# First stage of a two-layer diffusion backbone, reordered by K tiles

## The reference

```
sc  = silu(c);  scc = silu(c_ctx)
mod = s @ ada_w[i] + ada_b[i]                 # 6 chunks of 1024: shift, scale, gate, ...
h   = rms_norm(x, norm_mix[i]) * (1 + mod[1]) + mod[0]     # context with scc, latent with sc
proj = h @ w_in                               # 1024 -> 512 (cq) + 256 (ckv) + 32 (kr)
q  = rms_norm(cq, q_norm) @ w_uq
kv = rms_norm(ckv, kv_norm) @ w_ukv           # k_nope and v for 16 heads
kr = rope_2d(kr)                              # on the latent tokens
out = softmax(q k) v @ w_o
```

## Time and profile before

| | |
|---|---|
| median of three timed runs | 1244.3 us (1244.23 to 1246.67) |
| the profiled execution's own time | 1248.4 us |
| its span, first to last instruction | 1246.2 us |
| TensorE busy | 1162.3 us, 93% of the span |
| VectorE busy | 861.5 us, 69% |
| ScalarE busy | 610.2 us, 49% |
| GpSimd busy | 221.4 us, 18% |
| mean granted TensorE clock | 0.976 |

### The profile page before, as it was taken

One profiled execution on the slowest core, in us unless ns is written; L12 is line 12 of the kernel. 1 busy time (PEld: TensorE's weight loads), 2 busy tenths in 40 slices (PEclk: granted clock), 3 DMA queues, 4 the chain that ended last, 5 costly groups with the idle time before them and its releaser, 6 DMA issues.

```text
span 1246.2 us, 19292 instructions
## 1 busy us (share of the span) xinstructions
PE 1162.3 (93%) x6954; PEld 974.1 (78%) x6954; DVE 861.5 (69%) x1255; ACT 610.2 (49%) x1048; POOL 221.4 (18%) x166
## 2 busy tenths in 40 slices
PE   5799999898999999999999799998999897999997
PEld 3577776678988888878888778885777797999996
DVE  0896887975887777774665678885888656555453
ACT  3657887733532223232222555547577445666442
POOL 0201444422100000000111100004975211000010
PEclk9899999999999999999999999999999898999999
DMA  9533222240574555554452142221222243556562
GB/s 380 189 135 118 70 84 86 68 169 1 186 235 172 184 200 200 172 191 144 160 171 68 50 136 68 84 84 47 73 73 72 93 151 115 192 179 190 148 186 72
DMA packets 48175, 168.23 MB, mean 135 GB/s; under 512 B 5232, under 2 KB 6512, under 8 KB 47856
## 3 DMA queue, kind: packets, MB, share of 16 engines
q1 hardware_dynamic: 48112, 167.38, 40.4%
HBM read 166.31 MB, written 1.05 MB: 134 GB/s over the span
## 4 chain that ended last, share of the span: by engine, by line
PE 69%; DVE 16%; ACT 7%; issue 3%; DMA 1%; POOL 1%; SPq 1%; DVEq 0%; ACTq 0%
PE bank L1675 21%; PE bank L1677 20%; PE bank L1676 20%; DVE scratch L1456 5%; DVE w_lo L1087 3%; PE bank L2100 2%; ACT w_hi L607 2%; DMA raw<-in_w_in 1%; ACT scratch L912 1%; PE bank L2133 1%; DVE softmax_max L1258 1%; PE bank L2112 1%; ACT conv_in L909 1%; PE bank L2122 1%; DVE mla_h_lo L1278 1%
## 5 line engine op out<-in xcount | busy, mean ns | idle before, releaser
L1087 DVE TENSOR_TENSOR w_lo<-raw,w_hi 128x1024 fp32r<-128x1024 f32 (+1 forms) x226 | 277.3, 1229 | 159.7 <-ACT w_hi L607 159.5
L607 ACT ACTIVATE w_hi<-raw 128x1024 fp32r<-128x1024 f32 (+1 forms) x226 | 230.8, 1023 | 274.8 <-PE bank L1677 252.8
L1675 PE MATMUL bank<-ffn_h_lo,w_hi 128*128 128x256 f32 (+1 forms) x736 | 246.0, 334 | 9.3 <-DVE ffn_h_lo L1124 5.6
L1676 PE MATMUL bank<-ffn_h_hi,w_hi 128*128 128x256 f32 (+1 forms) x736 | 245.1, 333 | 0.0
L1677 PE MATMUL bank<-ffn_h_hi,w_lo 128*128 128x256 f32 (+1 forms) x736 | 245.0, 333 | 0.0
L1675 PEld LDWEIGHTS bank<-ffn_h_lo,w_hi 128*128 128x128 f32 x736 | 140.2, 191 | 25.2 <-issue 6.0
L1677 PEld LDWEIGHTS bank<-ffn_h_hi,w_lo 128*128 128x128 f32 x736 | 140.3, 191 | 14.5
L1676 PEld LDWEIGHTS bank<-ffn_h_hi,w_hi 128*128 128x128 f32 x736 | 140.3, 191 | 14.5
L462 POOL TENSOR_TENSOR scratch<-scratch 128x512 f32<-128x512 f32 (+1 forms) x24 | 34.6, 1441 | 618.8 <-ACT scratch L616 618.8
L1675 PE MATMUL bank<-ssd_h_lo,w_hi 128*128 128x256 f32 (+2 forms) x360 | 125.6, 349 | 4.5 <-DVE ssd_h_lo L1361 2.3
L1675 PE MATMUL bank<-ffn_hidden_lo,w_hi 128*128 128x256 f32 (+1 forms) x374 | 124.4, 333 | 5.8 <-DVE ffn_hidden_lo L1416 5.8
(11 more groups left out here) (265 smaller groups left out, 2159.2 us busy)
## 6 DMA issues: line engine op xcount, KB each, us to landing
raw<-in_w SPq DMA_DIRECT2D x120, 512.0 KB, 4.3
scratch<-in_vec_w SPq DMA_DIRECT2D x56, 512.0 KB, 3.6
vec_weights<-in_vec_w SPq DMA_DIRECT2D x24, 512.0 KB, 3.6
raw<-in_w_xbc SPq DMA_DIRECT2D x24, 512.0 KB, 3.5
ada_start<-in_ada_w SPq DMA_DIRECT2D x8, 1024.0 KB, 17.2
raw<-in_w_z SPq DMA_DIRECT2D x16, 512.0 KB, 3.5
raw<-in_w_so SPq DMA_DIRECT2D x16, 512.0 KB, 3.5
raw<-in_w SPq DMA_DIRECT2D x16, 384.0 KB, 3.9
```

The source lines that it names most:

```text
L607: A(wh[s % RING][:, 0:c], raw[s % RING][:, 0:c], ACT.Copy).then_inc(w_hi, 1)
L1087: V.tensor_tensor(wl[s % RING][:, 0:c], raw[s % RING][:, 0:c], wh[s % RING][:, 0:c].bitcast(f32), SUB).then_inc(w_lo, 1)
L1675: mm(o, lh, rl, start=first, stop=False)
L1676: mm(o, lh, rh, start=False, stop=False)
```

## The change

The order of the first stage is turned: K tiles outside, output tiles inside.

- adaLN columns are laid out anew: group q holds shift and scale of K tiles 2q and 2q+1. `start_mods(q)` copies the rows, waits for the turn, adds the bias and forms the gain of these two K tiles alone.
- X is loaded first, in two halves; TensorE's sums over X come ahead of all adaLN groups, and VectorE's reciprocal ahead of the first row copy.
- w_in is loaded by K tile: eight blocks of 128x896 in place of seven of 128x1024. All later blocks move by one number in the ring.
- The projection runs K tile by K tile into seven banks (`in_all(k)`, 21 matmuls each), with the adaLN groups and turns between; K tiles 6 and 7 are done last, output tile by output tile.
- In VectorE's list two matvecs stand before the fourth row copy and three behind it. ScalarE's silu of the c rows stands behind H's K tiles 4 and 5. Two weight blocks of the heads are split behind the loop over t.
- astart gets SBUF space of its own beside H, since both are now live together.

```diff
-            ada_start(0)
+            for i in range(2):
+                sp.dma_start(X[:, 4 * i:4 * i + 4, :], a["xT"][:, 4 * i:4 * i + 4, :]).then_inc(x_in[i], 16)
+            ada_start(0)
             sp.dma_start(tab[:, :], a["tab"]).then_inc(inputs_in, 16)
             ada_start(1)
-            sp.dma_start(X[:, :, :], a["xT"]).then_inc(x_in, 16)
             ada_start(2)
             ada_start(3)
+            load(IN, IN, 896, one("w_in", 0))
+            load(IN + 1, IN + 1, 896, one("w_in", 1))
             ada_start(4)
             ada_start(5)
...
+            load(IN + 4, IN + 4, 896, one("w_in", 4))
+            sp.dma_start(crow[:, :, :], a["crow"]).then_inc(crow_in, 16)
+            vec(0, vec_mla[:, 0, :])
+            vec(1, vec_mla[:, 1, :])
+            for t in range(5, 8):
+                load(IN + t, IN + t, 896, one("w_in", t))
```

ScalarE (`start_his(k)` makes the high part of K tile k, as `his_shared` did):

```diff
+            hi(IN, IN)
+            start_his(0)
+            hi(IN + 1, IN + 1)
+            act.wait_ge(in_gain, 1)
+            start_his(1)
+            for q in range(1, 4):
+                act.wait_ge(in_gain, q + 1)
+                start_his(2 * q)
+                start_his(2 * q + 1)
+                if q == 1:
+                    hi(IN + 2, IN + 2)
+                    hi(IN + 3, IN + 3)
+                if q == 2:
+                    hi(IN + 4, IN + 4)
+                    act.wait_ge(crow_in, 16)
+                    A(crow[:, :, :], crow[:, :, :], ACT.Silu).then_inc(crow_silu, 1)
+                    hi(IN + 5, IN + 5)
+                    hi(IN + 6, IN + 6)
+            hi(IN + 7, IN + 7)
+            hi(VB, VB)
+            hi(VB + 1, VB + 1)
...
             for t in range(7):
-                act.wait_ge(w_used, IN + t + 1)
+                if t < 6:
+                    act.wait_ge(in_mm, t + 1)
+                else:
+                    act.wait_ge(w_used, IN + KD)
```

VectorE:

```diff
+            dve.wait_ge(inv, 1)
+            for q in range(4):
+                start_mods(q)
+                start_value(2 * q)
+                if q == 0:
+                    lo(IN, IN)
+                start_low(2 * q)
+                start_low(2 * q + 1)
+                if q == 0:
+                    lo(IN + 1, IN + 1)
+                elif q == 1:
+                    lo(IN + 2, IN + 2)
+                    lo(IN + 3, IN + 3)
+                elif q == 2:
+                    lo(IN + 4, IN + 4)
+                    dve.wait_ge(crow_silu, 1)
+                    matvec_mla(0)
+                    lo(IN + 5, IN + 5)
+                    matvec_mla(1)
+                    lo(IN + 6, IN + 6)
+            matvec_mla(2)
+            lo(IN + 7, IN + 7)
+            matvec_mla(3)
+            lo(VB, VB)
+            matvec_mla(4)
+            lo(VB + 1, VB + 1)
             for t in range(7):
```

TensorE:

```diff
+            def in_all(k):
+
+                pe.wait_ge(w_lo, IN + k + 1)
+                pe.wait_ge(nlo, k + 1)
+                for t in range(7):
+                    if k == 0 and t >= 4:
+                        pe.wait_ge(*((row_cp, t - 3) if t < 6 else (root, 1)))
+                    last = in_part(k, t)
+                last.then_inc(w_used, 1)
+
+            ada_group(0)
+            pe.wait_ge(inputs_in, 16)
+            turn_ready(0)
+            turn()
+            ada_group(1)
+            in_all(0)
+            turn_ready(1)
+            turn()
+            in_all(1)
+            ada_group(2)
+            in_all(2)
+            turn_ready(2)
+            turn()
+            in_all(3)
+            ada_group(3)
+            in_all(4)
+            turn_ready(3)
+            turn()
+            in_all(5)
+            pe.wait_ge(w_lo, IN + KD)
+            for t in range(7):
+                for k in (6, 7):
...
             for g in range(8):
+                if g < 4:
+                    pe.wait_ge(proj_out, g + 3)
+                if 1 <= g < 4:
+                    pe.wait_ge(cq_lo, g)
...
                 if g == 0:
                     b = SQ[2]
+                    pe.wait_ge(cq_lo, KQ)
```

More of the change, by code:

```diff
@@ L93, in block_cols @@
     cols = [1024] * NBLK
+    for n in range(IN, IN + KD):
+        cols[n] = 896
     for n in range(HP, HP + 16):
@@ L734, in _, with start_his @@
-            act.wait_ge(crow_in, 16)
-            A(crow[:, :, :], crow[:, :, :], ACT.Silu).then_inc(crow_silu, 1)
+            def start_his(k):
+                even = k % 2 == 0
+                act.wait_ge(nv, NB[0] + k + 2) if even else act.wait_ge(nx, ODD[0] + k // 2 + 1)
+                for m, c0, c1 in ((1, 0, CTX), (0, CTX, TOK)):
+                    v = T[:, (2 if even else 6) + k // 2 % 2, c0:c1]
+                    if even:
+                        ins = A(Hmh[:, k, c0:c1], v, ACT.Identity, bias=mod[0][:, k, m:m + 1])
+                    else:
+                        ins = A(v, v, ACT.Identity, bias=mod[0][:, k, m:m + 1], scale=gain[0][:, k, m:m + 1])
+                if not even:
+                    ins.then_inc(nodd, 1)
+                    act.wait_ge(nodd, ODD[0] + k // 2 + 1)
+                    ins = A(Hmh[:, k, :], T[:, 6 + k // 2 % 2, :], ACT.Copy)
+                ins.then_inc(nhi, 1)
@@ L748, in _ @@
[L748 removed]
+                    square(2, k, bank[t][:, :])
+                    A(cnh[:, KKV + k, :], bank[t][:, :], ACT.Copy, scale=par[:, PAR["q_norm"] + k:PAR["q_norm"] + k + 1]).then_inc(proj_out, 1)
                 if t == 3:
@@ L1764, in _, with ada_group @@
             pe.wait_ge(silu_c, 1)
-            for g in range(4):
+            pe.wait_ge(ones_set, 3)
+            for k in range(KD):
+                pe.wait_ge(x_sq, k + 1)
+                last = mm(bank[6][:, :], ones[:, :], T[:, k, :], start=k == 0, stop=k == KD - 1)
+            last.then_inc(sum_done, 1)
+            def ada_group(g):
                 if g >= 2:
-                    pe.wait_ge(row_cp, g - 1)
+                    pe.wait_ge(mod_ev, g)
                 for r in range(2):
@@ L1770, in _ @@
                     for q in range(2):
-                        ada(4 * r + 2 * q, astart[:, 4 * g + 2 * r + q, :], bank[4 + g % 2])
-                if g == 0:
-                    pe.wait_ge(inputs_in, 16)
-                    pe.wait_ge(ones_set, 3)
-                if g == 1:
-                    for k in range(KD):
-                        pe.wait_ge(x_sq, k + 1)
-                        last = mm(bank[6][:, :], ones[:, :], T[:, k, :], start=k == 0, stop=k == KD - 1)
-                    last.then_inc(sum_done, 1)
@@ L1799, in _ @@
+            pe.wait_ge(w_lo, IN + KD)
+            for t in range(7):
+                for k in (6, 7):
+                    if t == 0:
+                        pe.wait_ge(nlo, k + 1)
+                    last = in_part(k, t)
+                    if t == 6 and k == 6:
+                        last.then_inc(w_used, 1)
+                last.then_inc(in_mm if t < 6 else w_used, 1)
+                if t in (1, 3):
+                    j = 1 if t == 1 else 2
                     if t == 1:
-                        pe.wait_ge(root, 1)
```

139 lines of the change are left out of this document (64 added, 75 removed).

## The result

The changed kernel takes 1250.5 us (median of 7 runs, 1249.8 to 1255.2); the kernel before took 1244.3 beside it (7 runs, 1242.3 to 1246.7). That is 6.2 us more between the medians. The ratio, which is formed from all runs and not from the two medians, is 1.0062, 95% interval 1.0041 to 1.0083: slower by 0.6%, clear of noise. The forecast was 1251.0. Four of the seven runs of after lie from 1249.8 to 1250.5 and three from 1254.9 to 1255.2. Its profiled execution is one of the long ones: 1255.2 us, with a span of 1253.5. The profiled execution of before, 1248.4 us with a span of 1246.2, is longer than all seven timed runs of before.

The account below looks back on a forecast made before the run. TensorE was taken as the bound from 43.15 us to V's end at 99.71. Terms 32.1 + 12.05 + 15.3 + 8.25 + 10.7 + 23.85, plus clock 4.2, gave 106.4: 6.7 us later, median 1251.0, range 1244 to 1257.

Parts of the forecast that it names:

- my own case: The main forecast, 1251.0 us for the median: chance 0.60, said to span 1247.5 to 1254 alone.
- A: End of K tile 0 in the projection, predicted at 32.1 us.
- B: Third turn, after K tile 1, an adaLN group and K tile 2: A + 12.05 us.
- C: Fourth turn, B + 15.3 us: TensorE stands still 3.3 us, the row copy being queued behind two matvecs.
- F: Start of the last two K tiles, C + 8.25 us, after TensorE stands still another 3.05 us for weights 7.
- The opening: Loads to first projection matmul: sums over X end at 16.0 us, matmul at 25.65, 17.5 us earlier than before.
- The clock: Half-clock stretches of 3.4 us behind idles, costing 1.7 us each: 1.7 charged at F, 2.5 at V.
- One to one behind V: Behind V only buffer numbers are edited, so V's 6.7 us delay carries unchanged into the total.
- Rival 1: Clock holds and sums run at full speed: V ends at 100.9, 1.2 us later, 1245.5; chance 0.12.
- Rival 3: Longer half stretches, sums at half speed throughout or two at F: 10 to 12 us later, 1255; chance 0.13.
- Rival 2: TensorE stays the bound, vector chain much shorter: V ends at 85.3, 1230, case put at 1238; chance 0.10.
- Rival 4: Clock falls at every K tile: four stretches of 1.7 us more, 6.8 on top, 1258; chance 0.05.

Follow-up runs that it names:

- experiment 8: Changed kernel with 12 unused matmuls of ones on ones ahead of the sums over X: 1252.4 us, ratio 1.0056 to the kernel before.
- experiment 4: Changed kernel with weights 5 and 6 and the fourth row copy ahead of all matvecs, silu behind their high parts, matvecs spread out later: 1247.1 us, ratio 1.0012.
- Experiment 1: Changed kernel with the fourth adaLN row copy alone moved ahead of the two matvecs: 1254.1 us, ratio 1.0068 to the kernel before.
- experiment 3: Changed kernel with unused matmuls in the two waits at V and four more of full width among the q sums: 1251.3 us, ratio 1.0045.
- experiment 6: Changed kernel with six V tiles, in banks 0 to 5, ahead of the q sums: 1246.9 us, ratio 1.0005 to the kernel before.
- experiment 2: Changed kernel with 21 unused matmuls ahead of V tile 0 and 17 behind it: 1250.9 us, ratio 1.0040 to the kernel before.
- experiment 7: Kernel before with the load of X alone moved ahead of the adaLN weights: 1245.7 us, ratio 1.0003 to the kernel before.
- experiment 9: Changed kernel with 12 and 6 unused matmuls around the first turn, to hold the opening's clock: 1251.1 us, ratio 1.0052 to the kernel before.
- experiment 12: Changed kernel with kv norm early, six V tiles ahead of q sums, row copies before matvecs, matvecs drawn into VectorE's waits, silu earlier: 1235.6 us, ratio 0.9929.

## Why the prediction was right, step by step

The forecast of 1251.0 was met by 1250.5, and the order of the waits, their releasers and the sign were those of the working. That the number was hit to 0.5 us is in part luck. The median is the uppermost of the four short runs, and the second measurement, with three short and three long runs, gave 1252.8. In the short run that was profiled V ended 2.0 us ahead of the forecast, and in the long one 2.0 us behind it. And some of the measured difference lies behind V, where the forecast had nothing.

Two sums of the prediction don't come out as written. The end of the sums over X is 16.1, not 16.0, which changes nothing. The span of my own case, given as 1247.5 to 1254, does not follow from its parts: with 0 to 5.1 us for the clock it is 1246.8 to 1251.9, and with 1.5 for the durations 1245.3 to 1253.4.

By its own terms, with both profiled executions of after:

| term | predicted | 1255.2 us run | 1249.7 us run |
|---|---|---|---|
| first projection matmul | 25.65 | 26.58 | 25.40 |
| K tile 0 (to A) | 6.45 | 6.47 | 4.96 |
| A to B | 12.05 | 12.33 | 12.34 |
| B to C (fourth turn) | 15.3 | 15.28 | 15.27 |
| C to F (last two K tiles) | 8.25 | 8.52 | 8.37 |
| F to the kv reciprocal, clock at F in it | 12.4 | 10.88 | 10.89 |
| reciprocal to V's end, clock at V in it | 26.35 | 28.35 | 27.13 |
| V's end | 106.4 | 108.41 | 104.36 |

**The opening.** Right in order, a little short in one term. The sums took 9.84 us and not 8.8, so by the 7.1 of full speed they ran at half speed for some 5.4 us (an estimate) and not 3.4; in the other profiles of edits of after it was 8.54 to 10.15, but for the 7.10 of experiment 8. The value beside GpSimd's products took 1.86 us and alone 0.88; I had charged 2.15 and 0.84.

**The chain by K tiles.** The two middle terms were hit to 0.3 us. The mechanism is shown twice: the copy follows the second matvec in the trace, and experiment 4, which takes both matvecs from ahead of the copy, removes the wait and returns 3.4 us of the median of after (1250.5), 5.7 of that of its second measurement, or 0.5% by the ratios to the kernel before. Experiment 1 adds that the wait at the turn was not a cost of its own. It was one of two places where TensorE waits for the same total of VectorE's work, and undoing it alone made one long idle of two short ones.

**The clock.** Two terms were mis-sized, in opposite directions. At F I charged 1.7, and in these two profiles it cost nothing: the half stretch fell from 60.4 to 63.8 in the long one, on K tile 5, for which TensorE had time (its wait ahead of the last K tiles became 1.79 instead of my 3.05). Other executions show that this is not fixed: in the profiles of experiments 3 and 6, which are unedited up to F, a half stretch also fell from about 70 to 74 us, and from F to the reciprocal it took 12.5 us, as charged. At V I charged 2.5: the q sums and the seven V tiles took 15.8 us in the long run against the 11.6 of my working, so 4.2, which is above my bound of 3.4. In the short run they took 14.6, so 3.0. I had taken stretches of 3.4 us, one or two; it was one of 17.1 in the long run and of 13.6 in the short one, where waits of 5.41 and 3.34 us stand with six matmuls between them. Experiment 3 shows the size from the other side: with the clock at 1.00 there, V ends 12.6 us behind the start of the sums, 0.9 of it for four more matmuls. With one stretch of 3.4 us left, in experiment 2, it is 13.2. The rest of V's term, reciprocal to q sums, was 12.5 against 12.25.

**One to one behind V.** This step is the weakest. The first scores follow V by 10.15 us in both kernels, and the remainder is 1136.3 us before and 1134.9 in the long run of after. But the profile of before is of a run above all timed ones: behind its V the clock stands at half for 44 us in all. In the run of 1244.1 us of experiment 7, the kernel before with X first, that is 34 us and the remainder 1131.7. The short run of after, also with 34 us at half there, has 1133.4, and the long one, with 41 us, 1134.9. Short run against short run, V ends 4.3 us later (104.36 and 100.08) and the remainder is 1.6 us longer. Long run against that same short one, it is 8.3 and 3.2 us. So about a quarter of the loss lies behind the first scores, and what makes it there was not looked into. Carrying V's end one to one from the long profile of before onto the median of before was sound in sign and not to a microsecond.

**The rivals.** Rival 1, the clock holds, did not come about by itself, and holding it by force in one place (experiments 2, 3 and 9) leaves the kernel 0.40 to 0.52% slower than before. No kernel held it everywhere, so how far the waits alone carry the loss was not measured. Rival 3, longer stretches, had the number of the upper group, 1255, but not its places: I had put them at the sums to their end (14.2 us) and at F, and they came at V, by 8.7 us for V's end and not 10 to 12. I had given 1251 and 1255 as cases; they turned out to be two ways in which one kernel runs. Rival 2, TensorE stays the bound, is false for this order. Experiment 12, which needs the three chains undone and the matvecs placed, comes near it: V's end at 89.11 against the rival's 85.3, with 4.7 us of TensorE's idle time left on the way. Rival 4 was not seen: from 33 to 40 us, up to the border of K tiles 1 and 2, the granted clock is 1.00, the idle at that border is 0.28 us, and no half stretch falls from 30.0 us to the fourth turn at 60.66. The Trainium skill (TensorE: Matmul & The Clock Gate, HAM oscillation) warns of a wait before each K tile. By that rule the trace agrees: with K outside but hardly a wait, nothing falls; behind the waits of 3.15 and 5.41 us it did. K outside by itself cost no clock here.

**What stays open.** The runs of after form two groups 5 us apart. In the two profiles the waits are alike and the places of the half stretches are not, and with the opening's clock held (experiment 9) or V's (experiment 2) the upper group is absent in five runs each. It is absent from the six runs of experiment 8 as well (1251.1 to 1253.1), whose clock fell in the opening and at V, so this doesn't prove either place the cause. In experiment 3, where V's clock was held too, it is present, with one half stretch more around the kv norm. What decides at which waits the stretches fall in an execution I did not settle. Nor did I separate how much of experiment 4's return is the silu's place and how much the matvecs'.

## What to carry to other kernels

When a loop order moves the start of a stage forward, the total follows only if each in-order queue that feeds the stage is re-sorted by when its results are needed; work without haste belongs in an engine's own waits, neither ahead of an urgent copy nor all at the end (here 16.6 us were won at the start, TensorE stood still for 14 us behind it, and re-sorting the lists with the same K loops made the kernel 15 us faster). Undoing a single wait can be worth nothing when the next one has the same source: sum the feeding engine's list, not the bound engine's waits. And short waits close together should be costed with the clock: here 10 to 17 us at half for two of them, not 3.4 for each. A comparison that rests on one profile of each kernel should take executions near the two medians.

## What the runs showed of the hardware that I had not expected

- The q sums behind a wait of 0.73 us (experiment 2), with TensorE busy for 2.56 of the 3 us around them, were followed by 3.4 us at half. With four 512-column matmuls among them behind a wait of 0.74 (experiment 3), or with no wait before them (the kernel before), by none. That is one profile of each.
- Waits of 5.41 and 3.34 us with six matmuls between gave 10.2 to 17.1 us at half around V (five kernels); waits of 2.71 and 0.88 gave 10.2; a wait of 2.68 with no second one near it (experiment 12) gave none.
- The same kernel has runs at 1250 and at 1255 with the same waits. The Trainium skill says of a kernel's start (TensorE: Matmul & The Clock Gate, "What's actually happening") that the number of matmuls that run slowly varies between runs of one kernel. The trace agrees: the first sums of after took 9.84 us in one profile and 8.91 in the other. That is 0.9 of the 5.6 us between them; the rest lies further on.
- Matmul rate did not suffer from going round seven banks with every third matmul: 0.233 us from one to the next inside K tile 0 of the short run, as before (0.235).
